# Probabilities times values in two halves around the state and output updates of the middle stage

## The chip, the cores and the metric

The kernel runs on one core of one Trainium2 chip. Its time is the device time of one execution in microseconds (us). The profile names five engines: PE (TensorE, with PEld for its weight loads), DVE (VectorE), ACT (ScalarE), POOL (GpSimd) and SP (SyncE, which only issues transfers here).

## What is computed

One layer of a streaming encoder: a layer norm, an input projection, two groups of heads side by side, an output projection with a layer norm, and an MLP with another. The change touches the place where the two groups of heads share TensorE. Cut to that:

```python
# (a) gated delta rule, per head: state S, blocks of tokens
u = U_c - jnp.einsum('bhck,bhkv->bhcv', W_c, S)
o = jnp.einsum('bhck,bhkv->bhcv', qd_c, S) + jnp.einsum('bhij,bhjv->bhiv', qk_c, u)
S = gt_c[..., None, None] * S + jnp.einsum('bhck,bhcv->bhkv', kd_c, u)
# (b) attention over a sliding window, with a sink per head
s = jnp.einsum('bnqhgd,bnshd->bnhgqs', q, k).astype(jnp.float32) * SWA_HD ** -0.5 + bias
p = jax.nn.softmax(jnp.concatenate([s, sink], axis=-1), axis=-1)[..., :-1]
return jnp.einsum('bnhgqs,bnshd->bnqhgd', p.astype(v.dtype), v)
# then o is normalised per head and gated; both groups are concatenated
h = layer_norm(DEEP_ALPHA * h + mix @ w_o, ln1_g, ln1_b)
```

Sizes: 2048 prompt tokens, 16 meta tokens and 32 sample tokens, 8 heads of width 64 in each group, model width 1024, everything float32.

## The kernel before

Three stages follow each other: the projection (`project_stage`, to about 690 us), the middle stage (`mix_stage`, to about 1420 us) and the MLP (`mlp_stage`, the rest). The middle stage walks over 18 tiles of 128 tokens. Each engine has a function `step(t)`, which lists its work for tile t in a fixed order, and `over_tiles` runs it: four tiles written out, then a hardware loop of two tiles a turn, then four more. Tile 17 holds the sample tokens. An engine does its list strictly in this order. Between engines stand semaphores: `pe.wait_ge(s["u_done"], ...)` holds TensorE until VectorE has written `u`.

The tiles are skewed. While tile t goes through the delta rule, the next tile n = t + 1 is prepared (gates, decays, scores) and the tile before, p = t - 1, gets its output product and layer norm. So one `step(t)` of TensorE runs: the gates and transposes of n; `turn_o(p)` (the transposes of the normalised `o` of tile p, which wait for `on_done`); `turn_queries(n)`; half of the output product of p; `from_state(t)`; and so on down to the part that matters here:

- `scores(n)` (L1109): scores of the next tile, into the banks `fr` and `inv`.
- `solve_rest(t)` (L1181): the last step of the triangular solve, into `one1`.
- `attend(t)` (L1232): probabilities times values of the 8 heads, two matmuls a head, into the bank `pair`.
- `state_update(t)` (L1188), which waits for `u_done`, and `output_update(t)` (L1194), which has the same input `u`, into `one1` and `one2`.
- `turn_attention(t)` (L1239): 4 transposes of the scaled attention, which wait for `attn_scaled`.
- `turn_values(n)` (L1118): 2 transposes of the next tile's values into `one2`, which wait for `o_done`, since `one2` must have been read.
- then the next step begins with `turn_gates` (L1032).

VectorE at the same place: `biased(n)` (L1458, 8 heads, waits for the scores), `update(t)` (L1519 writes `u`, then L1520), `maxima(n)`, `norm_stats(p)`, `new_state(t)` (L1530), `scale_attention(t)` (L1565, waits for `pv_full`, which `attend` gives), `norm_shift(p)` (L1589), `new_output(t)` (L1525, waits for `oin_full`, which `output_update` gives, and gives `o_done`). Its next step begins with `copy_gates`, `copy_sums` (L1386 to L1394) and `sum_squares` (L1535).

ScalarE: `norm_rstd(p)`, `normalise(p)` (L1797, waits for `norm_shift`), `square_o(t)` (L1765, waits for `o_done`), `mix_attention(t)` (L1777, waits for `turn_attention`), `split_attention(t)` (L1783), `copy_values(n)` (L1749).

In the steps of tiles 0 and 16 `maxima(n)` also hides keys (`hide`, L1465 and L1473), which takes VectorE some 5 us more.

Of the kernel before, what the change touches and what calls it, by code (L numbers as in the profile page):

```python
# [35 lines left out]
HEADS, HD = 8, 64  # L36
# [677 lines left out]
def by(t, per, k=None):  # L714

    return t.n * per + (per if k is None else k)
# [12 lines left out]
def mix_stage(nc, ctx, io, project):  # L729
# [69 lines left out]
    def heads4(ps, n=P):  # L799
        return ps[:, :].rearrange("p (h c) -> p h c", c=n)  # L800
# [22 lines left out]
    s = {n: m.sem(n) for n in names}  # L823
# [16 lines left out]
    def following(t):  # L840

        return None if t.last() else t.plus(1)
# [179 lines left out]
    def _(pe):  # L1022
# [30 lines left out]
        def turn_queries(t):  # L1053
            if t.reaches(2):
                pe.wait_ge(s["attn_mixed"], by(t.plus(-2), 1))
            pass_waits(pe, s["passed"])
            turn_rows(t, pair, 0, s["q_turned"])
# [54 lines left out]
        def turn_values(t):  # L1112
            if t.reaches(1):
                pe.wait_ge(s["o_done"], by(t.plus(-1), 1))
            else:
                pe.wait_ge(*project.evacuated)
            for j in range(2):
                last = pe.transpose(one2[:, j * P:j * P + P], values[:, j * P:j * P + P], ident)  # L1118
            last.then_inc(s["vwin_turned"], 1)
# [97 lines left out]
                last = pe.transpose(out, probs[:, h, j * P:j * P + P], ident)  # L1217
            last.then_inc(s["pt_full"], 1)

        def attend(t):  # L1220
            pe.wait_ge(s["vwin_copied"], by(t, 1))
            pe.wait_ge(s["pt_copied"], by(t, 2))
            if t.reaches(2):
                pe.wait_ge(s["h1t_copied"], by(t.plus(-2), 2))
            elif t.reaches(1):
                pe.wait_ge(s["attn_mixed"], by(t.plus(-1), 1))
            if not t.last():
                pe.wait_ge(s["squared"], by(t.plus(1), 2))
            for h in range(HEADS):
                kv = h // 4  # L1230
                for j in range(2):
                    last = pe.matmul(pair[:, h * HD:h * HD + HD], probs_t[:, j, h, :], v_rows[:, j, kv * HD:kv * HD + HD],  # L1232
                                     start=j == 0, stop=j == 1)
            last.then_inc(s["pv_full"], 1)

        def turn_attention(t):
            pe.wait_ge(s["attn_scaled"], by(t, 1))
            for j in range(4):
                last = pe.transpose(pair[:, j * P:j * P + P], attn[:, 2 * j:2 * j + 2, :].rearrange("p a b -> p (a b)"), ident)  # L1239
            last.then_inc(s["ost_full"], 1)  # L1240
# [35 lines left out]
        def step(t):  # L1276
            n, p, pp = following(t), t.plus(-1), t.plus(-2)
            chain, norm = t.reaches(1), t.reaches(2)
            if n:
                turn_gates(n)  # L1280
                turn_rows(n, inv[1], 4, s["k_turned"])
                turn_rows(n, inv[0], 8, s["v_turned"])
                sum_gates(n)
                mask_future(n)
                spread_gates(n)
            if chain:
                turn_o(p)
            if n:
                turn_queries(n)
            if chain:  # L1290
                output_product(p, 0, ATTENTION, n)
            if n:
                key_products(n)
            from_state(t)
            if chain:
                output_product(p, 0, DELTA)
            if n:
                query_products(n)
            if chain:
                output_product(p, 1, ATTENTION)  # L1300
            if norm:
                turn_h1(pp, 0, n)
            turn_probs(t, 0)
            pair_rows(t)
            turn_probs(t, 1)
            pair_update(t)
            if norm:
                turn_h1(pp, 1)
            if chain:
                output_product(p, 1, range(0, 2))  # L1310
            solve_head(t)
            if chain:
                output_product(p, 1, range(2, 4))
            carry_over(t)
            if n:
                scores(n)
            solve_rest(t)
            attend(t)
            state_update(t)
            output_update(t)  # L1320
            turn_attention(t)
            if n:
                turn_values(n)

        def first_turns():
            relative_bias()
# [36 lines left out]
    def _(dve):  # L1363
# [158 lines left out]
        def new_output(t):  # L1522
            dve.wait_ge(s["oin_full"], by(t, 1))
            dve.wait_ge(s["qs_scaled"], by(t, 2))
            dve.tensor_tensor(o[:, :, :], o[:, :, :], heads4(one2, HD), ALU.add).then_inc(s["o_done"], 1)  # L1525
# [36 lines left out]
        def scale_attention(t):  # L1562
            dve.wait_ge(s["pv_full"], by(t, 1))
            dve.wait_ge(s["soft_end"], by(t, 2))
            dve.tensor_tensor(attn[:, :, :], heads4(pair, HD), across(soft[:, 5, :], HD), ALU.mult).then_inc(s["attn_scaled"], 1)  # L1565
# [39 lines left out]
        def step(t):  # L1605
            n, p = following(t), t.plus(-1)
            chain = t.reaches(1)
            if n:
                copy_gates(n)
                copy_sums(n)  # L1610
            if chain:
                sum_squares(p)
                low(p, ATTENTION, 1)
                normalise_o(p)
            if n:
                sum_keys(n)
            if chain:
                gate_o(p)
            if t.reaches(2):
                norm_gain(t.plus(-2))  # L1620
            if n:
                strengths(n)
                scale_values(n)
            if chain:
                low(p, DELTA, 2)
            if n:
                decayed_keys(n)
            residue(t)
            if chain:
                residual(p, 0)  # L1630
            if n:
                left_keys(n)
                decayed_queries(n)
                sum_queries(n)
            turn_even(t)
            copy_pair_rows(t)
            place_pair(t)
            if chain:
                residual(p, 1)
            take_over(t)  # L1640
            softmax_sums(t)
            if n:
                biased(n)
            update(t)
            if n:
                maxima(n)
            if chain:
                norm_stats(p)
            new_state(t)
            scale_attention(t)  # L1650
            if chain:
                norm_shift(p)
            new_output(t)
            if not chain:
                for k in DELTA:
                    split_wo(k)
# [32 lines left out]
    def _(act):  # L1689
# [57 lines left out]
        def copy_values(t):  # L1747
            act.wait_ge(s["vwin_turned"], by(t, 1))
            act.activation(v_rows[:, :, :], one2[:, 0:SPAN].rearrange("p (a c) -> p a c", c=P), ACT.Copy).then_inc(s["vwin_copied"], 1)  # L1749
# [13 lines left out]
        def square_o(t):  # L1763
            act.wait_ge(s["o_done"], by(t, 1))
            act.activation(o_sq[:, :, :], o[:, :, :], ACT.Square).then_inc(s["o_squared"], 1)  # L1765
# [7 lines left out]
        def mix_attention(t):  # L1773
            act.wait_ge(s["ost_full"], by(t, 1))
            if t.reaches(1):
                act.wait_ge(s["mix_lo_done"], by(t.plus(-1), 2, 1))
            act.activation(mixed[:, 4:8, :], heads4(pair), ACT.Copy).then_inc(s["attn_mixed"], 1)  # L1777
# [26 lines left out]
        def step(t):  # L1804
            n, p, pp = following(t), t.plus(-1), t.plus(-2)
            chain, norm = t.reaches(1), t.reaches(2)
            if n:
                square_keys(n)
            if chain:
                rstd_o(p)  # L1810
            if n:
                decays(n)
                key_norms(n)
            if chain:
                split_delta(p)
            if n:
                square_queries(n)
            probabilities(t, range(0, 3))
            if n:
                to_lanes(n)  # L1820
            probabilities(t, range(3, HEADS))
            if n:
                query_norms(n)
            if norm:
                copy_h1(pp, 0)
            copy_probs(t, 0)
            copy_probs(t, 1)
            if norm:
                copy_h1(pp, 1)
            copy_head(t)  # L1830
            if chain:
                norm_rstd(p)
                normalise(p)
            square_o(t)
            mix_attention(t)
            split_attention(t)
            if n:
                copy_values(n)
            if not chain:
                for k in DELTA:  # L1840
                    split_wo(k)
# [531 lines left out]
```

## Time and profile before

| | |
|---|---|
| median of 3 runs | 2953.55 us (2951.76 to 2960.93) |
| the profiled execution, its own time | 2953.84 us |
| its span | 2952.0 us |
| PE busy | 2743.6 us, 93% |
| DVE, ACT, POOL busy | 44%, 31%, 45% |
| mean granted clock of TensorE | 0.964 |

The page shows one execution. Busy shares are means over stages, so the stretch of the middle stage is read by itself: the waits of one engine, and the instructions of each engine in order of time. In a row of the timeline the first number is the start, the second the time to the end of the last instruction of the group, and the brackets hold the idle time ahead of it and what ended it. A group of matmuls ends a little after the next one starts, because matmuls overlap. Every product of two float32 operands here has two records, so 16 records are 8 products.

### The profile page before, as it was taken

The page shows a single profiled execution, that of the slowest core. Times are in us where ns is not written, and L with a number is a line of the kernel's source. Part 1 is how long each engine was busy: PE and PEld are TensorE (multiplying, and loading weights), DVE is VectorE, ACT ScalarE, POOL GpSimd, SP SyncE. Part 2 cuts the span into 40 slices and gives each one's busy share as a digit, 9 for nine tenths or more (in the row PEclk, how much of TensorE's full clock was granted, in tenths as well). Part 3 has the DMA queues.
Part 4 walks back from the last instruction along what each step waited for, and adds up shares of the span by engine and source line. Part 5 has one row for each costly group of instructions (what it writes and reads, how often), then busy time and mean ns, then how long its engine had stood idle before and what let it go on. Part 6 is the DMA issues. An engine that isn't in the chain of part 4 may idle for free.

```text
span 2952.0 us, 50987 instructions
## 1 busy us (share of the span) xinstructions
PE 2743.6 (93%) x17652; PEld 2600.4 (88%) x17652; DVE 1287.8 (44%) x2442; ACT 922.6 (31%) x1966; POOL 1333.6 (45%) x1840
## 2 busy tenths in 40 slices
PE   5899988977999999998599999999999999999996
PEld 5799988966888877887499999999999999999996
DVE  7634420016766667765344126413641364136402
ACT  4322241113444444443122222222222222222222
POOL 4200003002555544553255555555555555555553
PEclk9899999986999999998799999999999999999998
DMA  5322243232343333332334434443443344434433
GB/s 195 122 93 70 70 91 88 69 134 76 96 111 106 106 105 96 96 105 73 112 118 139 125 111 136 152 125 112 135 151 125 114 135 150 126 115 136 140 116 86
DMA packets 225941, 336.70 MB, mean 114 GB/s; under 512 B 78426, under 2 KB 161562, under 8 KB 223018
## 3 DMA queue, kind: packets, MB, share of 16 engines
q1 hardware_dynamic: 205210, 331.44, 36.5%
q10 hardware_dynamic: 20640, 4.07, 0.7%
q8 instruction: 54, 0.88, 0.1%
q14 instruction: 37, 0.30, 0.0%
HBM read 265.67 MB, written 69.78 MB: 114 GB/s over the span
## 4 chain that ended last, share of the span: by engine, by line
PE 50%; DVE 1%; DMA 0%; issue 0%; ACTq 0%; DVEq 0%
PE c_bank L128 16%; PE c_bank L130 16%; PE c_bank L129 16%; PE c_turned L2088 1%; DMA c_out<-scratch_h_cols 0%; DVE c_stats L2212 0%; DVE c_raw L2209 0%; DVE c_h_lo L2254 0%; DVE c_out L2248 0%; DVE c_raw L2261 0%; DVE c_h_hi L2252 0%; DVE c_raw L2264 0%; DVE c_mean_var L2215 0%; ACTq L2133 0%; DVEq L2248 0%
## 5 line engine op out<-in xcount | busy, mean ns | idle before, releaser
L2123 POOL TENSOR_TENSOR c_w_lo<-c_raw,c_w_hi 128x512 fp32r<-128x512 f32 x640 | 852.8, 1333 | 641.7 <-ACT c_w_hi L2143 641.7
L2143 ACT ACTIVATE c_w_hi<-c_raw 128x512 fp32r<-128x512 f32 x640 | 404.4, 632 | 1056.9 <-PE c_bank L130 1025.1
L128 PE MATMUL c_bank<-c_h_hi,c_w_hi 128*128 128x416 f32 x1280 | 453.6, 354 | 24.8 <-POOL c_w_lo L2123 23.0
L130 PE MATMUL c_bank<-c_h_hi,c_w_lo 128*128 128x416 f32 x1280 | 452.2, 353 | 0.0
L130 PE MATMUL c_bank<-c_mid_hi,c_w_lo 128*128 128x416 f32 x1280 | 450.8, 352 | 0.0
L128 PE MATMUL c_bank<-c_mid_hi,c_w_hi 128*128 128x416 f32 x1280 | 450.2, 352 | 0.0
L129 PE MATMUL c_bank<-c_h_lo,c_w_hi 128*128 128x416 f32 x1280 | 448.6, 350 | 0.0
L129 PE MATMUL c_bank<-c_mid_lo,c_w_hi 128*128 128x416 f32 x1280 | 447.0, 349 | 0.0
L2248 DVE COPY c_out<-c_bank 128x416 f32 x40 | 23.7, 591 | 627.3 <-PE c_bank L130 627.3
L1895 POOL TENSOR_TENSOR b_lane_t<-b_lane_a,b_lane_n 128x60 f32<-128x60 f32 (+24 forms) x558 | 160.2, 287 | 297.3 <-DMA b_lane_a<-scratch_at_lanes 255.0
L128 PEld LDWEIGHTS c_bank<-c_h_hi,c_w_hi 128*128 128x128 f32 x1280 | 241.4, 189 | 27.1 <-POOL c_w_lo L2123 24.6
L130 PEld LDWEIGHTS c_bank<-c_h_hi,c_w_lo 128*128 128x128 f32 x1280 | 241.3, 189 | 3.3
L129 PEld LDWEIGHTS c_bank<-c_h_lo,c_w_hi 128*128 128x128 f32 x1280 | 241.1, 188 | 2.8
L130 PEld LDWEIGHTS c_bank<-c_mid_hi,c_w_lo 128*128 128x128 f32 x1280 | 240.2, 188 | 3.2
L129 PEld LDWEIGHTS c_bank<-c_mid_lo,c_w_hi 128*128 128x128 f32 x1280 | 240.0, 188 | 2.8
L128 PEld LDWEIGHTS c_bank<-c_mid_hi,c_w_hi 128*128 128x128 f32 x1280 | 240.4, 188 | 0.1
L567 POOL TENSOR_TENSOR a_w_lo<-a_raw,a_w_hi 128x1024 fp32r<-128x1024 f32 x20 | 48.2, 2412 | 393.2 <-ACT a_w_hi L586 393.2
L2195 DVE TENSOR_SCALAR c_positive<-c_bank 128x416 f32<-128x416 f32 x160 | 94.4, 590 | 242.9 <-PE c_bank L130 242.9
L128 PE MATMUL a_one<-a_h_hi,a_w_hi 128*128 128x420 f32 (+1 forms) x480 | 171.1, 356 | 15.3 <-ACT a_row L613 15.3
L1898 POOL TENSOR_TENSOR b_lane_n<-b_lane_n,b_lane_t 128x60 f32<-128x60 f32 (+24 forms) x558 | 159.2, 285 | 43.7
L129 PE MATMUL a_one<-a_h_lo,a_w_hi 128*128 128x420 f32 (+1 forms) x480 | 170.3, 355 | 0.0
L130 PE MATMUL a_one<-a_h_hi,a_w_lo 128*128 128x420 f32 (+1 forms) x480 | 170.3, 355 | 0.0
(277 smaller groups left out, 4654.2 us busy)
## 6 DMA issues: line engine op xcount, KB each, us to landing
c_raw<-in_w_ff SPq DMA_DIRECT2D x320, 512.0 KB, 3.7
scratch_proj<-a_row SPq DMA_DIRECT2D x22, 1152.0 KB, 5.1
b_qkv<-scratch_proj SPq DMA_DIRECT2D x18, 768.0 KB, 6.5
a_raw<-in_w_in SPq DMA_DIRECT2D x23, 512.0 KB, 5.9
a_x<-in_x SPq DMA_DIRECT2D x18, 512.0 KB, 3.6
scratch_h_rows<-a_h SPq DMA_DIRECT2D x18, 512.0 KB, 2.7
b_lane_a<-scratch_at_lanes SPq DMA_DIRECT2D x72, 128.0 KB, 2.7
b_res<-scratch_h_rows SPq DMA_DIRECT2D x18, 512.0 KB, 3.3
```

Of the source, the lines that this page charges most:

```text
L128: pe.matmul(out, w_hi, x_hi, start=first, stop=False)
L129: pe.matmul(out, w_hi, x_lo, start=False, stop=False)
L130: return pe.matmul(out, w_lo, x_hi, start=False, stop=last)
L567: pool.tensor_tensor(w_lo[:, p, :, :], raw[:, p, :, :], w_hi[:, p, :, :].bitcast(F32), ALU.subtract).then_inc(w_lo_done, 1)
L1895: pool.tensor_tensor(term, lane_a[:, j, j + 1:SMALL].unsqueeze(1).to_broadcast(shape), lane_n[:, 0:n, j].unsqueeze(2).to_broadcast(shape), ...
L1898: last = pool.tensor_tensor(here, here, term, ALU.add)
L2088: last = pe.transpose(turned[p][0:TOK, c * P:c * P + P], out[:, c, i * TOK:i * TOK + TOK], ident[:, :])
L2123: pool.tensor_tensor(w_lo[:, p % 2, ks, :], raw[:, p, ks, :], w_hi[:, p % 2, ks, :].bitcast(F32), ALU.subtract).then_inc(w_lo_done, 1)
L2143: act.activation(w_hi[:, p % 2, ks, :], raw[:, p, ks, :], ACT.Copy).then_inc(w_hi_done, 1)
L2195: dve.tensor_scalar(positive[:, :], src, 0.0, None, ALU.max).then_inc(positive_done, 1)
L2248: dve.tensor_copy(out[:, one(c2 * 2 + c), :], bank2[c][:, 0:BLOCK].unsqueeze(1)).then_inc(out_done, 1)
```

## The change

TensorE does heads 0 to 3 of `attend` ahead of `state_update`, and heads 4 to 7 behind `output_update`. All waits of `attend` stand ahead of the first half; `pv_full` is given by the second. `turn_values` moves ahead of `turn_attention`. VectorE does `new_output` right behind `new_state`, and `scale_attention` last in the step. ScalarE does `copy_values` ahead of `mix_attention`.

```diff
-        def attend(t):
-            pe.wait_ge(s["vwin_copied"], by(t, 1))
-            pe.wait_ge(s["pt_copied"], by(t, 2))
-            if t.reaches(2):
-                pe.wait_ge(s["h1t_copied"], by(t.plus(-2), 2))
-            elif t.reaches(1):
-                pe.wait_ge(s["attn_mixed"], by(t.plus(-1), 1))
-            if not t.last():
-                pe.wait_ge(s["squared"], by(t.plus(1), 2))
-            for h in range(HEADS):
+        def attend(t, heads):
+            if heads[0] == 0:
+                pe.wait_ge(s["vwin_copied"], by(t, 1))
+                pe.wait_ge(s["pt_copied"], by(t, 2))
...
+            for h in heads:
...
-            last.then_inc(s["pv_full"], 1)
+            if heads[-1] == HEADS - 1:
+                last.then_inc(s["pv_full"], 1)
...
-            attend(t)
+            attend(t, range(0, 4))
             state_update(t)
             output_update(t)
-            turn_attention(t)
+            attend(t, range(4, HEADS))
             if n:
                 turn_values(n)
+            turn_attention(t)
...
             new_state(t)
-            scale_attention(t)
+            new_output(t)
             if chain:
                 norm_shift(p)
-            new_output(t)
+            scale_attention(t)
...
             square_o(t)
+            if n:
+                copy_values(n)
             mix_attention(t)
             split_attention(t)
-            if n:
-                copy_values(n)
```

On TensorE, at the end of a step inside the loop, from the last score to the first transposes of the next step (the line numbers shift by one or two in the changed kernel):

```order
 L1109 MATMUL a_inv<-b_keys,b_sq 128x256
 L1181 MATMUL a_one<-b_rn,b_nn_1005 64x64 x8
-L1232 MATMUL a_pair<-b_v_rows,b_probs_t 128x64 x16
+L1233 MATMUL a_pair<-b_v_rows,b_probs_t 128x64 x8
 L1188 MATMUL a_one<-b_u,b_kd_1010 64x64 x8
 L1194 MATMUL a_one<-b_u,b_qk_1008 128x64 x8
-L1239 MATMUL a_pair<-b_masks,b_turned_rows 128x128 x4
+L1233 MATMUL a_pair<-b_v_rows,b_probs_t 128x64 x8
 L1118 MATMUL a_one<-b_masks,b_values 128x128 x2
+L1241 MATMUL a_pair<-b_masks,b_turned_rows 128x128 x4
 L1032 MATMUL a_prod<-b_masks,b_gate_rows 128x16
```

Half of the attention's matmuls now stand between the output update and the value transposes, and the attention transposes (L1239, now L1241) come last.

VectorE at the end of the same step, before:

```order
311 L1519 TENSOR_TENSOR b_u<-a_one,b_neg_beta 128x512
312 L1520 TENSOR_TENSOR b_state<-b_state,b_e_end 128x256
...
316 L1585 BN_AGGR b_mean_var<-b_stats 128x2
317 L1530 TENSOR_TENSOR b_state<-b_state,a_one 128x256
318 L1565 TENSOR_TENSOR b_turned_rows<-a_pair,b_soft 128x512
319 L1589 SCALAR_TENSOR_TENSOR b_small<-b_mean_var,b_small 128x1
320 L1525 TENSOR_TENSOR b_o<-b_o,a_one 128x512
321 L1386 COPY b_gate<-a_prod 128x2x8
```

and in the changed kernel, where every line number of VectorE is three higher:

```order
311 L1522 TENSOR_TENSOR b_u<-a_one,b_neg_beta 128x512
312 L1523 TENSOR_TENSOR b_state<-b_state,b_e_end 128x256
...
316 L1588 BN_AGGR b_mean_var<-b_stats 128x2
317 L1533 TENSOR_TENSOR b_state<-b_state,a_one 128x256
318 L1528 TENSOR_TENSOR b_o<-b_o,a_one 128x512
319 L1592 SCALAR_TENSOR_TENSOR b_small<-b_mean_var,b_small 128x1
320 L1568 TENSOR_TENSOR b_turned_rows<-a_pair,b_soft 128x512
321 L1389 COPY b_gate<-a_prod 128x2x8
```

The new output (L1525, now L1528) and the scaled attention (L1565, now L1568) have changed places; what writes `u` has the 8 instructions of `biased(n)` ahead of it in both.

## Rows read from the trace of the kernel before

**Rows 1.** The page: PE's busy time, its share of the span, instructions.

```profile
PE 2743.6 (93%) x17652; PEld 2600.4 (88%) x17652; DVE 1287.8 (44%) x2442; ACT 922.6 (31%) x1966; POOL 1333.6 (45%) x1840
```

**Rows 2.** Waits of PE, 780 to 1300 us: total, times, longest.

```profile
PE a_one L1201 <- DVE b_turned_rows L1546: 15.0, 13, 1.2
PE a_one L1118 <- DVE b_o L1525: 4.4, 13, 0.3
PE a_fr L1071 <- DVE b_cum L1394: 3.8, 13, 0.3
```

**Rows 3.** Timeline of PE, end of one step: start, length, line [idle before].

```profile
1028.49 1.14 PE L1181 MATMUL a_one<-b_rn,b_nn 64*64 64x64 f32 x16
1029.56 3.79 PE L1232 MATMUL a_pair<-b_v_rows,b_probs_t 128*128 128x64 f32 x32
1033.27 0.97 PE L1188 MATMUL a_one<-b_u,b_kd 128*64 128x64 f32 x16
1034.17 2.00 PE L1194 MATMUL a_one<-b_u,b_qk 128*128 128x64 f32 x16
1036.00 0.61 PE L1239 MATMUL a_pair<-b_masks,b_turned_rows 128*128 128x128 f32 x4
1036.95 0.44 PE L1118 MATMUL a_one<-b_masks,b_values 128*128 128x128 f32 x2 [0.34 <-DVE b_o L1525]
1037.32 0.23 PE L1032 MATMUL a_prod<-b_masks,b_gate_rows 16*128 16x16 f32 x1
...
1041.98 0.66 PE L1201 MATMUL a_one<-b_masks,b_turned_rows 128*128 128x128 f32 x4 [1.11 <-DVE b_turned_rows L1546]
```

**Rows 4.** Timeline of DVE, the same step.

```profile
1028.77 0.48 DVE L1458 CUSTOM_DVE_ANT_0 b_probs<-a_fr,b_bias,b_sinks 128x256 f32<-128x256 f32 x1 [0.98 <-PE a_inv L1109]
...
1032.02 0.69 DVE L1519 TENSOR_TENSOR b_u<-a_one,b_neg_beta 128x512 f32<-128x512 f32 x1
...
1034.89 0.40 DVE L1530 TENSOR_TENSOR b_state<-b_state,a_one 128x256 f32<-128x256 f32 x1
1035.21 0.68 DVE L1565 TENSOR_TENSOR b_turned_rows<-a_pair,b_soft 128x512 f32<-128x512 f32 x1
1035.81 0.15 DVE L1589 SCALAR_TENSOR_TENSOR b_small<-b_mean_var,b_small 128x1 f32<-128x1 f32 x1
1036.20 0.69 DVE L1525 TENSOR_TENSOR b_o<-b_o,a_one 128x512 f32<-128x512 f32 x1 [0.25 <-PE a_one L1194]
...
1039.48 0.68 DVE L1535 TENSOR_REDUCE b_o_sum<-b_turned_rows 128x8 f32<-128x512 f32 x1
```

**Rows 5.** Timeline of ACT, the same step.

```profile
1035.99 1.24 ACT L1797 ACTIVATE b_x<-b_x,b_small 128x1024 f32<-128x1024 f32 x1 [0.45 <-DVE b_small L1589]
1037.14 0.61 ACT L1765 ACTIVATE b_turned_rows<-b_o 128x512 f32<-128x512 f32 x1
...
1038.34 0.63 ACT L1783 ACTIVATE b_mix_hi<-b_mixed 128x512 fp32r<-128x512 f32 x1
```

**Rows 6.** Timeline of PE, the attention transposes in tiles 0 and 16.

```profile
712.63 1.08 PE L1239 MATMUL a_pair<-b_masks,b_turned_rows 128*128 128x128 f32 x4 [2.80 <-DVE b_turned_rows L1565]
...
1356.00 1.12 PE L1239 MATMUL a_pair<-b_masks,b_turned_rows 128*128 128x128 f32 x4 [4.55 <-DVE b_turned_rows L1565]
```

**Rows 7.** Windows of PE: stretch, us, busy (instructions), granted clock, DMA share, GB/s.

```profile
840.00:850.00 10.00, 8.78 (x80) 0.83 0.25 48
...
1280.00:1290.00 10.00, 10.00 (x76) 0.86 0.21 31
```

**Rows 8.** Timeline of PE, first output product of two tiles and what follows.

```profile
1002.80 0.75 PE L128 MATMUL a_prod<-b_wo_hi,b_mix_hi 128*128 128x512 f32 x1
...
1007.32 1.16 PE L1081 MATMUL a_fr<-b_qkv 64*128 64x128 f32 x16
...
1042.83 0.48 PE L128 MATMUL a_prod<-b_wo_hi,b_mix_hi 128*128 128x512 f32 x1
...
1045.77 1.16 PE L1081 MATMUL a_fr<-b_qkv 64*128 64x128 f32 x16
```

More of the change, by code:

```diff
@@ L1218, in turn_probs @@
             last.then_inc(s["pt_full"], 1)
-        def attend(t):
-            pe.wait_ge(s["vwin_copied"], by(t, 1))
-            pe.wait_ge(s["pt_copied"], by(t, 2))
-            if t.reaches(2):
-                pe.wait_ge(s["h1t_copied"], by(t.plus(-2), 2))
-            elif t.reaches(1):
-                pe.wait_ge(s["attn_mixed"], by(t.plus(-1), 1))
-            if not t.last():
-                pe.wait_ge(s["squared"], by(t.plus(1), 2))
-            for h in range(HEADS):
+        def attend(t, heads):
+            if heads[0] == 0:
+                pe.wait_ge(s["vwin_copied"], by(t, 1))
+                pe.wait_ge(s["pt_copied"], by(t, 2))
+                if t.reaches(2):
+                    pe.wait_ge(s["h1t_copied"], by(t.plus(-2), 2))
+                elif t.reaches(1):
+                    pe.wait_ge(s["attn_mixed"], by(t.plus(-1), 1))
+                if not t.last():
+                    pe.wait_ge(s["squared"], by(t.plus(1), 2))
+            for h in heads:
                 kv = h // 4
```

## The prediction

> **What bounds the kernel now.** The page comes first: TensorE is busy for 93% of the span, every other engine for less than half [rows 1]. So time comes only out of TensorE's gaps, and is lost wherever it gets a new one. The waits of TensorE in 13 middle tiles come second [rows 2]: `turn_o` waits 15.0 us in all (1.15 us a tile) for the normalised `o`; `turn_values` 4.4 us (0.34) for `o_done`; `spread_gates` 3.8 us (0.29). There is nothing else. In particular there is no wait for `u_done` and none for `attn_scaled`. The timeline tells why [rows 3, 4]. The last score is followed by VectorE's `biased`, from 1028.77 to 1032.02, and `u` is written from 1032.02 to 1032.71. TensorE is meanwhile in `attend`, from 1029.56 to 1033.27, 3.71 us long. `u` is there 0.56 us before TensorE asks for it: `attend` is the cover for `biased` and `u`, and nearly all of it is needed.
>
> **The change part by part**, for one tile in the middle (tiles 1 to 15 run alike), on the clock times of [rows 3, 4]. The matmuls are the same, so only waits are to be found.
>
> First half of `attend`: half of 3.71 is 1.85 us, so it ends at 1031.41. `u` is ready at 1032.71, and from the end of `new_output` at 1036.89 to the start of L1118 at 1036.95 a release takes 0.06, so `state_update` starts at 1032.77. That is a new wait of 1.36 us, which the 0.56 us of slack don't cover. Everything behind it in TensorE's queue stands still.
>
> State update 0.90 us (1033.27 to 1034.17) and output update 1.83 us (1034.17 to 1036.00), so they end at 1035.50, 0.50 us sooner than before. Second half of `attend`: 1.85 us, to 1037.35. `new_output` needs the output update's last result (2.00 us after its start, 1035.67) and VectorE, which is free at 1035.3 behind `new_state` (its input comes at about 1033.7, and L1530 is held till 1034.89 by the statistics, as before). So it runs from 1035.70 to 1036.39, and `turn_values` no longer waits: the 0.34 us are gone. It takes 0.37 us (1036.95 to 1037.32), to 1037.72.
>
> `turn_attention` now waits for `scale_attention`, which waits for the second half. Its last result comes some 0.16 us after TensorE could go on (2.00 against 1.83), at 1037.51; VectorE starts 0.03 later, takes 0.68 us [rows 4] and is seen 0.06 later: 1038.28. TensorE has been idle since 1037.72, a second new wait of 0.56 us. Before, the scaling was over at 1035.89, when TensorE was still in the output update. The transposes take about 0.44 us, so the next step's `turn_gates` starts at 1038.72 instead of 1037.32: **1.40 us later**. As a sum of gaps: 1.36 + 0.56 - 0.34 = 1.58, of which the earlier 0.34 is measured from the end of a group and not from where the next could start (0.5 us from there: 1036.95 less 1036.44); start to start it is 1.40, which I keep.
>
> Does the rest of the step give it back? The one large wait is `turn_o`'s. It waits for a chain that begins at VectorE's L1535. That instruction starts at 1039.48, right behind `copy_sums`, although its input, the squares, was ready at 1037.75 [rows 5]. So the chain hangs on the gates of the next tile, which TensorE itself starts, and moves with them by 1.40 us. That `o` is ready sooner brings nothing. ScalarE's part gets later and stays covered: `norm_shift` now stands behind `new_output`, so `normalise` starts at about 1036.5 instead of 1035.99, the squares are ready at 1038.25 instead of 1037.75, and L1535 would now start at 1040.9. `copy_values` (0.3 us) ahead of `mix_attention` fills a time in which that one waits anyway: it can start only at 1038.9, `split_attention` ends at about 1040.1, and VectorE takes the low part only behind L1535, so after 1041.6. The next `copy_gates` finds VectorE free since 1038.22. No transfer is moved; no queue of SP or POOL is passed.
>
> The other tiles. In steps 0 and 16 VectorE is 5 us late by `hide`, and TensorE waits for it at the attention's transposes [rows 6]. The halves move inside these 2.80 and 4.55 us. The new order adds the 0.6 us of L1525 ahead of the scaling, but `turn_values` goes in ahead of it and covers that: 0 for tile 0, 0.3 us for tile 16. Tile 17 has no `biased`, so `u` comes in time; its attention ends 0.1 us later. Sum: 15 x 1.40 + 0.4 = **21.4 us**.
>
> **The clock** is the open term. The granted clock falls to its lower level (1.2 instead of 2.4 GHz) for a short stretch after `turn_o`'s wait in 8 of the 15 tiles: 8 stretches between 740 and 1340 us, of which the windows of the first and the last stand in [rows 7]. Its price: from the first output matmul to `key_products` one such tile takes 4.52 us, one at full clock 2.94 [rows 8], so 1.58 us. The old waits stay as they are and come 1.4 us later, so the 8 can become anything from 0 to 15: -12.6 to +11.1 us. The new wait of 1.36 us is about as long as `turn_o`'s (1.1 to 1.2), after which the clock does fall in half the cases. But `turn_o`'s has a second wait (L1071) shortly ahead of it [rows 2], and the new one stands between dense matmuls. It can cost a second stretch in 0 to 15 tiles, 0 to 23.7 us. Of all this I take three stretches more, 4.7 us, near the lower end, because the nearest rows with a single gap don't show it.
>
> Total: 2953.84 + 21.4 + 4.7 = 2980 us. The profiled execution is 0.3 us from the median of the runs, so no correction.
>
> One rule from outside speaks on the price of a wait. The trace shows at L1118 that the transposes' first weights were loaded when the wait ended, not during it: both start at 1036.95, as they must if the wait stands ahead of both. The Trainium skill, page "TensorE: Matmul & The Clock Gate", section "Step-by-step: what each phase is for", says that TensorE pulls weight loads ahead of matmuls still in flight. If that also passed a semaphore wait, each of the two new waits would be cheaper by one load, at the page's P / 1.2 some 0.1 us (an estimate), and the sum smaller by 3 us. By this trace it doesn't.
>
> **The rivals.**
> *The clock falls in nearly every tile behind the new wait.* For: its length. Against: the dense work on both sides. With 12 to 15 more stretches instead of 3 the sum is 21.4 + 19 to 24: 2994 to 2999 us. Chance 0.18.
> *`u` comes sooner than by the row.* Its place is `biased`: if its eight instructions ran faster while TensorE did less beside them, and `u` were there by 1031.41 (1.30 us sooner, which is the point from which this decides), the step would be 0.90 + 1.83 + 1.85 + 0.16 + 0.03 + 0.68 + 0.06 + 0.44 from there: 1037.36, +0.04 us a tile, 2955 us. Half of it gives 2965. Against: the eight take 0.41 us each from 1028.77 to 1032.02, and no row shows that TensorE slows them. Chance 0.07.
> *`turn_o` follows the output update instead of the gates.* Then the earlier `o` counts, the wait of 1.11 us a tile goes, and with it the fall of the clock behind it: 21.4 - 16.6 - 12.6 = -7.8, 2946 us. It decides if L1535 is held by the squares. The rows show it held by the queue. Chance 0.03.
> *The half behind the output update doesn't land where it should*, since its results and the scaling lie in one bank and ScalarE gets late by more than I count: another 0.5 us a tile, 2987 us. Chance 0.07.
>
> **How the numbers follow.** The forecast has a chance of 0.65, with its own range of 2968 to 2990 (21.4 with 5 fewer up to 9 more stretches). To hold the time 8 times in 10, the range takes in most of the clock rival: 2966 to 2996. A measurement here can tell about 0.3% (9 us) from no change, so "slower" begins at 2962.4: forecast, clock rival, late half, and half of the second rival, 0.91. Within 0.3%: 0.07. Faster: 0.02.
>
> **What the new profile would show.** A wait of TensorE at the state update for `u` of 1.2 to 1.4 us in 15 tiles; one at the attention's transposes for the scaling of 0.4 to 0.6 us; none at `turn_values`; `turn_o` unchanged at 1.1 to 1.2. No wait for `u` would make the first step wrong; a shorter `turn_o` wait the claim on the chain. The count of stretches at half clock decides the last term.

## The result and the profile after

The changed kernel takes 3060.34 us (median of 4 runs, 3048.28 to 3070.0) against 2957.24 (2951.76 to 2966.41): a ratio of **1.0343, interval 1.0296 to 1.0391**. Slower, as forecast, but by 103 us where 26 were forecast, and outside the range. The profiled execution is the slowest of the four, 3070.0 us.

The waits of TensorE in the whole middle stage (where, waited for whom, total, times, longest):

```profile
PE a_one L1188 <- DVE b_u L1522: 19.9, 17, 1.2
PE a_one L1201 <- DVE b_turned_rows L1549: 16.1, 17, 3.1
...
PE a_pair L1241 <- DVE b_turned_rows L1568: 6.7, 17, 0.8
...
PE a_one L1118 <- DVE b_o L1528: 0.3, 1, 0.3
```

Two waits are new and one is gone, as the step by step working said: for `u` (L1188), for the scaled attention (L1241), and no longer for `o_done` at L1118 [rows 2]. `turn_o` (L1201) waits 1.0 to 1.2 us in 10 of the tiles 1 to 15, as before, and less in the others. The two new ones are 27 us, so waits are not where 103 us went. The timeline of TensorE over the end of one step, to be read beside [rows 3]:

```profile
1033.98 2.00 PE L1233 MATMUL a_pair<-b_v_rows,b_probs_t 128*128 128x64 f32 x16
1037.17 1.60 PE L1188 MATMUL a_one<-b_u,b_kd 128*64 128x64 f32 x16 [1.19 <-DVE b_u L1522]
1038.70 3.68 PE L1194 MATMUL a_one<-b_u,b_qk 128*128 128x64 f32 x16
1042.17 3.62 PE L1233 MATMUL a_pair<-b_v_rows,b_probs_t 128*128 128x64 f32 x16
1045.59 0.63 PE L1118 MATMUL a_one<-b_masks,b_values 128*128 128x128 f32 x2
1046.58 1.12 PE L1241 MATMUL a_pair<-b_masks,b_turned_rows 128*128 128x128 f32 x4 [0.36 <-DVE b_turned_rows L1568]
1047.62 0.28 PE L1032 MATMUL a_prod<-b_masks,b_gate_rows 16*128 16x16 f32 x1
...
1053.64 1.07 PE L1201 MATMUL a_one<-b_masks,b_turned_rows 128*128 128x128 f32 x4 [1.22 <-DVE b_turned_rows L1549]
```

From start to start, the state update takes 1.53 us (0.90 before), the output update 3.47 (1.83), the second half of the attention 3.42 (1.85 by half of before). From the state update to `turn_gates` it is 10.45 us; the forecast had 5.95. Windows of the same stretch (us, busy and instructions of PE, granted clock, DMA share, GB/s) show the reason:

```profile
1033.00:1036.00 3.00, 2.98 (x32) 1.00 0.21 86
1036.00:1039.00 3.00, 1.83 (x18) 0.61 0.00 0
1039.00:1042.00 3.00, 3.00 (x16) 0.50 0.00 0
1042.00:1045.00 3.00, 3.00 (x16) 0.50 0.00 0
1045.00:1048.00 3.00, 2.64 (x12) 0.50 0.09 25
1048.00:1051.00 3.00, 2.97 (x14) 0.61 0.65 171
1051.00:1054.00 3.00, 1.52 (x18) 0.95 0.22 33
1054.00:1057.00 3.00, 3.00 (x12) 0.50 0.22 33
1057.00:1060.00 3.00, 3.00 (x25) 0.98 0.00 0
```

The clock falls to half in the wait for `u` and stays there over all that follows, 13.7 us, into the gates of the next tile. It falls once more behind `turn_o`'s wait. A long stretch comes in 14 of the tiles 1 to 15 (not in tile 3). It begins between 0.5 us before and 2.0 us after the start of the state update and lasts 10.2 to 20.5 us; in 8 of the 14 tiles a second, short one of 3.4 us follows. A tile takes 46.5 us on average instead of 39.5. Counts and lengths of stretches, here and below, are read from the granted clock over tiles 1 to 15 of the one profiled execution of each kernel; the windows shown are examples. Over the same 600 us the mean granted clock is 0.83 against 0.98 in the kernel before:

```profile
740.00:1340.00 600.00, 566.26 (x4819) 0.83 0.32 87
```

Where the time of such a tile goes, start to start, in us:

| part of the tile | before | after | forecast |
|---|---|---|---|
| start of the attention to start of the state update | 3.71 | 3.19 | 3.21 |
| state update to `turn_gates` | 4.05 | 10.45 | 5.95 |
| `turn_gates` to `turn_o` | 4.66 | 6.02 | 4.66 |

### The profile page after: what moved, and what is told of

Same layout as the page of the kernel before. It is cut to its first block and busy times, and to the rows that moved or that the text cites. A ratio compares the mean times of both kernels' runs of the same rounds, so it can differ in the third digit from the quotient of the medians.

```text
span 3068.2 us, 50987 instructions
## 1 busy us (share of the span) xinstructions
PE 2853.2 (93%) x17652; PEld 2698.7 (88%) x17652; DVE 1289.9 (42%) x2442; ACT 927.5 (30%) x1966; POOL 1331.8 (43%) x1840
```

## The experiments

Theory A: TensorE's idleness in the wait for `u` makes the clock fall, and the light work behind it (matmuls of 64 columns, each behind its own weight load, and transposes) keeps it low. Theory B: the light work, now in one piece, makes it fall however long the wait is. Theory C: the wait at the attention's transposes does it. All ratios are to the kernel before on the same chip, which took 2953 to 2961 us; so kernels of different groups are compared by their ratios.

**Six heads ahead, two behind.**

```diff
-            attend(t, range(0, 4))
+            attend(t, range(0, 6))
...
-            attend(t, range(4, HEADS))
+            attend(t, range(6, HEADS))
```

> The changed kernel with 6 heads ahead of the state update and 2 behind the output update. The same matmuls and the same order otherwise; only the wait for u gets shorter, from 1.2 us (shown) to about 0.3, since 2.78 us of attention cover it instead of 1.85. Theory A (the wait for u makes the clock fall, and the light work behind it keeps it low): no fall at the state update, some 7 us over the kernel before by the waits alone, 2961 to 2966 us, ratio to before about 1.002 to 1.004. Theory B (the clock falls because the light matmuls now lie in one piece with the transposes, however long the wait is): still 3040 to 3060 us. Theory C (it is the wait at the attention's transposes, which stays at 0.4 to 0.6 us here): also above 3030 us.

Measured: 2974.35 us, ratio 1.0073 (1.0056 to 1.009). Waits of TensorE, 780 to 1300 us (where, for whom, total, times, longest):

```profile
PE a_one L1201 <- DVE b_turned_rows L1549: 15.0, 13, 1.2
PE a_pair L1241 <- DVE b_turned_rows L1568: 6.0, 13, 0.5
PE a_one L1188 <- DVE b_u L1522: 3.9, 13, 0.3
```

The wait for the scaling is still there, 0.5 us a tile, the wait for `u` is 0.3, and the clock falls at the state update in none of the 15 tiles. That is against C and B. The time is 8 us above the range expected, 2961 to 2966, and the ratio above its 1.004: the short stretches behind `turn_o` rose from 8 to 12 tiles, which the expectation had left out.

**The new order without the split.**

```diff
-            attend(t, range(0, 4))
+            attend(t, range(0, HEADS))
             state_update(t)
             output_update(t)
-            attend(t, range(4, HEADS))
```

> All 8 heads ahead of the state update as before, but the rest of the change kept: new output ahead of the scaled attention, value transposes ahead of the attention's, the value copy first on ScalarE. It shows what the new order costs without the split. Wait for u: none. The attention's transposes wait for the scaling, which now comes 0.7 us later: +0.7 us a tile, 10 us, 2964 to 2968 us. Theory A: no long stretch at half clock, ratio about 1.003 to 1.005. Theory B and C: long stretches here too, since the light work and the wait at the transposes are both there, above 3030 us.

Measured: 2982.14 us, ratio 1.0092 (1.0075 to 1.0109), above my 2964 to 2968. The waits are 0.8 us a tile at the value transposes and 0.2 at the attention's. The expectation had only 0.7 at the attention's; it did not say that the value transposes, now ahead, wait for `o_done`. And the short stretch behind `turn_o` comes in all 15 tiles, with one more in tile 1. There is no long stretch: against B, and less strongly against C, whose wait is only 0.2 us here. So even the order by itself is a loss.

**`u` ahead of the biased scores.** The layer norm's statistics go ahead with it.

```diff
-            if n:
-                biased(n)
-            update(t)
-            if n:
-                maxima(n)
             if chain:
                 norm_stats(p)
+            update(t)
+            if n:
+                biased(n)
+                maxima(n)
```

> The changed kernel with 4 and 4 heads, but VectorE does the layer norm's statistics and the update (which writes u) ahead of the biased scores. u is then there 0.7 us after the solve, at about a third of the first half of the attention, so the wait for u is gone; the biased scores end 0.7 to 0.9 us later, ahead of where they are needed. Theory A: no fall at the state update; the step is as long as before to 0.1 us, 2955 to 2965 us, ratio 1.000 to 1.003. Theory B or C: 3030 us and more.

Measured: 2968.0 us, ratio 1.0049 (1.0033 to 1.0066), 3 us above the range expected. Waits of TensorE, 780 to 1300 us:

```profile
PE a_one L1201 <- DVE b_turned_rows L1549: 15.0, 13, 1.2
PE a_pair L1241 <- DVE b_turned_rows L1568: 7.3, 13, 0.6
PE a_fr L1071 <- DVE b_cum L1397: 3.7, 13, 0.3
```

The split is as in the changed kernel, the wait for `u` is gone, and with it the long stretches: none in 15 tiles. What is left is the wait at the attention's transposes (0.6 us, now the only new wait) and short stretches in 10 tiles instead of 8.

**Work in place of the wait.**

```diff
+        def fill(p):
+            pe.wait_ge(s["resid_done"], by(p, 2))
+            for k in range(5):
+                pe.matmul(prod[:, :], mix_hi[:, 0, :], wo_hi[:, 0, 0:512], start=True, stop=True)
...
             attend(t, range(0, 4))
+            if chain:
+                fill(p)
             state_update(t)
```

> The changed kernel with 5 matmuls of 512 columns put between the first half of the attention and the state update, about 1.15 us of work whose result is never read, in tiles 1 to 17. The wait for u turns into work of the same length, and nothing else moves. Theory A (it is TensorE's idleness there): the clock keeps up at the state update and what is left is the pure delay that was forecast, 21 us: 2972 to 2980 us, ratio 1.006 to 1.009. Theory B (the light work behind it is enough): 3045 to 3065 us, as without the filling.

Measured: 2982.57 us, ratio 1.0099 (1.0083 to 1.0116). That is 3 us above the range expected, and by the ratios some 72 us less than the changed kernel, with more work in it. TensorE's timeline in one tile:

```profile
1046.69 2.00 PE L1233 MATMUL a_pair<-b_v_rows,b_probs_t 128*128 128x64 f32 x16
1048.50 1.40 PE L1241 MATMUL a_prod<-b_wo_hi,b_mix_hi 128*128 128x512 f32 x5
1049.89 0.97 PE L1188 MATMUL a_one<-b_u,b_kd 128*64 128x64 f32 x16
1050.79 2.00 PE L1194 MATMUL a_one<-b_u,b_qk 128*128 128x64 f32 x16
1052.62 1.95 PE L1233 MATMUL a_pair<-b_v_rows,b_probs_t 128*128 128x64 f32 x16
1054.41 0.39 PE L1118 MATMUL a_one<-b_masks,b_values 128*128 128x128 f32 x2
1055.36 0.66 PE L1246 MATMUL a_pair<-b_masks,b_turned_rows 128*128 128x128 f32 x4 [0.56 <-DVE b_turned_rows L1575]
1055.94 0.23 PE L1032 MATMUL a_prod<-b_masks,b_gate_rows 16*128 16x16 f32 x1
```

The state update starts 3.20 us after the attention, as in the changed kernel (3.19), so the data moves as there. But the clock is at full height through the updates, and they take 0.90 and 1.83 us. No tile of the 15 has a long stretch; 10 have the short one behind `turn_o`. From the attention to the gates it is 9.25 us; the prediction had 9.16. Its windows (columns as above):

```profile
1048.00:1052.00 4.00, 4.00 (x39) 1.00 0.00 0
1052.00:1056.00 4.00, 3.44 (x31) 1.00 0.00 0
1056.00:1060.00 4.00, 3.23 (x32) 1.00 0.57 148
1060.00:1064.00 4.00, 3.39 (x12) 0.57 0.30 46
```

Here dense work stands in the place of the idleness; with six heads ahead, and with `u` first, the idleness is gone and nothing dense was put in. The clock holds in all three. Together they settle that it is idleness, and not the order, that makes the clock fall at the state update.

**The wait without the split.** On the kernel before:

```diff
             if n:
                 biased(n)
-            update(t)
-            if n:
                 maxima(n)
             if chain:
                 norm_stats(p)
+            update(t)
```

> The kernel before, undivided attention and its own order, with one edit: VectorE writes u behind the maxima and the layer norm's statistics instead of ahead of them, 1.8 us later. TensorE then waits about 1.3 us for u (a gap of 1.1 to 1.2 us as the profile counts it), with no split. Theory A (the wait makes the clock fall, the light work behind it keeps it low up to the next output product): half clock from the state update on in most of the tiles, 10 to 14 us long, 3020 to 3050 us, ratio 1.023 to 1.033. Rival (only together with the split, with its second half of the attention behind, does the clock stay low): a fall of 3.4 us at most, 20 us of waits and 24 of clock, below 3000 us.

Measured: 3015.66 us, ratio 1.0195 (1.0177 to 1.0214), below the 3020 to 3050 of theory A and above the rival's 3000. The clock falls at the state update in 12 of 15 tiles, so a wait of about 1.3 us (1.2 to 1.4 in these 12 but for one of 1.6) is enough, split or not. Windows of one tile, whose state update starts at 1061.4:

```profile
1060.00:1063.00 3.00, 1.74 (x25) 1.00 0.00 0
1063.00:1066.00 3.00, 3.00 (x16) 0.50 0.00 0
1066.00:1069.00 3.00, 3.00 (x15) 0.50 0.21 62
1069.00:1072.00 3.00, 2.42 (x21) 0.86 0.63 149
```

But the stretch is 6.8 us in 10 of these tiles and 13.7 in 2. The expectation of 10 to 14 us was wrong, and so was its rival of 3.4. In the ten tiles the clock comes back 1.6 to 4.2 us after `turn_gates` starts; in the changed kernel, where the stretch is 10.2 or 13.7 us, 2.7 to 4.3 us after it. So it comes back at about the same place of the program, but without the second half of the attention that place comes sooner, and the fall itself comes 0.8 to 2.2 us after the update's start. By this reading, which no run tests alone, the split costs twice: it opens the wait, and it puts more light work behind it.

**Five heads ahead, three behind.** As the first diff, with 5 for 6.

> The changed kernel with 5 heads ahead and 3 behind: a wait for u of about 0.9 us (shown as 0.7), between that of 6 heads (shown 0.3, no fall) and that of 4 (shown 1.2, a fall in nearly every tile). If the fall comes with the length of the wait, gradually: falls at the state update in some tiles and 2985 to 3030 us. If it needs a wait near 1.2 us: none, and 14 us of delay plus what the stretches behind the normalised o cost with 6 heads: 2975 to 2985 us.

Measured: 2994.55 us, ratio 1.0107 (1.0085 to 1.0129), as expected for a fall that comes by degrees. A wait for `u` of 0.7 to 0.8 us made the clock fall at the state update in 3 of 15 tiles, and then for 13.7, 20.5 and 20.5 us; such a tile takes 45 to 47 us, one of the others 39.5 to 42.7. So the fall comes with the wait's length by degrees: 0 of 15 tiles at 0.3 us, 3 at 0.7, 14 at 1.2. The 3 were counted in the slowest of four executions; the others took 2984 to 2995 us, and no trace shows their falls.

**Dense work behind the state update.** The changed kernel with `fill` of 8 matmuls between the two updates; the wait for `u` is left.

```diff
             state_update(t)
+            if chain:
+                fill(p)
             output_update(t)
```

> The changed kernel, 4 and 4 heads, the wait for u left as it is, with 8 matmuls of 512 columns (never read) between the state update and the output update. They cost 1.8 us at full clock and 3.4 at half. Theory A (the clock falls by the wait, and stays low because what follows is light): it still falls in nearly every tile, but the stretch is 3.4 to 6.8 us instead of 13.7, and in spite of the added work the time is 3000 to 3035 us, below the changed kernel. Rival (the stretch has a length of its own, whatever work follows): 13.7 us as before, and 3080 us or more.

Measured: 3033.11 us, ratio 1.0248 (1.0231 to 1.0265), as expected by theory A, and by the ratios some 28 us less than the changed kernel although it does more. The clock still falls at the state update, in 14 of 15 tiles, but for 3.4 us in 12 of them and 6.8 in 2. One of the 12:

```profile
1026.00:1029.00 3.00, 2.16 (x18) 0.65 0.00 0
1029.00:1032.00 3.00, 3.00 (x16) 0.78 0.00 0
1032.00:1036.00 4.00, 3.44 (x31) 1.00 0.00 0
```

So the length of the stretch is no fixed price. It is set by what TensorE does at the low clock: 3.4 us with eight matmuls of 512 columns in it, 13.7 with light ones. And the light work behind the filling ran at full clock (last window), so light work alone does not bring the clock down.

**Only one of the two large waits.** The changed kernel, with the squares of `o` summed earlier:

```diff
             if n:
                 copy_gates(n)
-                copy_sums(n)
             if chain:
                 sum_squares(p)
+            if n:
+                copy_sums(n)
+            if chain:
                 low(p, ATTENTION, 1)
```

> The changed kernel with the squares of o summed early (between the gate copies), so that the wait for the normalised o falls from 1.2 to about 0.3 us, and the wait for u stays at 1.2. If the wait for u alone starts the stretch at half clock and light work carries it: it still falls in nearly every tile, 10 to 14 us long, and the time is the changed kernel's less 13 us or a little more: 3035 to 3050 us, ratio 1.025 to 1.03. If the two waits together made it (the clock kept down by the second): stretches of 6.8 us or less and 3000 us or below.

Measured: 3021.38 us, ratio 1.0222 (1.02 to 1.0243). By the ratios that is some 36 us less than the changed kernel, where 13 or a little more were expected. `turn_o` waits 0.3 us or less instead of 1.2, and the stretch at the state update is still there in 12 of 15 tiles, 10.2 us in 4 and 13.7 in 8. So it needs the wait for `u` alone. What is gone are the second, short stretches, which 8 tiles of the changed kernel had behind a long one, and the long ones of 17 and 20 us, which 4 had: these came with the other wait.

**The same edit on the kernel before, and on the split without its wait.**

> The kernel before with one edit: VectorE sums the squares of o between its copies of the gates and of their sums, in a gap of 1.2 us in which it waits, instead of behind them. The chain to the normalised o gets about 0.85 us shorter, so the one large wait of TensorE falls from 1.1 to 0.3 us a tile: 13 us. If the falls of the clock behind that wait (8 of 15 tiles, 1.6 us each) are due to it, they go too: 2928 to 2935 us, ratio 0.992 to 0.994. If they stay: 2940 us. If ScalarE's logarithm and exponential for o come no sooner, since it transposes squares first: 2950 us.

Measured: 2938.45 us, ratio **0.9923 (0.9903 to 0.9942)**: faster than both kernels, and the ratio is in the range expected (the time is 3 us above it, since the kernel before took 2961 us in this group). In the kernel before VectorE sat idle for 1.2 us between the two groups of copies:

```profile
1039.00 0.29 DVE L1391 COPY b_cum_row<-a_prod 72x128 f32<-72x128 f32 x1 [1.17 <-PE a_prod L1063]
```

Now it does the sum (L1535) there, right behind the gate copies:

```profile
1030.65 0.18 DVE L1386 COPY b_gate<-a_prod 128x16 f32<-128x16 f32 x1 [0.69 <-PE a_prod L1032]
1030.74 0.16 DVE L1387 COPY b_beta<-a_prod 128x8 f32<-128x8 f32 x1
1030.81 0.68 DVE L1535 TENSOR_REDUCE b_o_sum<-b_turned_rows 128x8 f32<-128x512 f32 x1
1031.52 0.18 DVE L1538 TENSOR_TENSOR b_o_sum<-b_o_sum,b_q_scale 128x8 f32<-128x8 f32 x1
1032.07 0.29 DVE L1391 COPY b_cum_row<-a_prod 72x128 f32<-72x128 f32 x1 [0.36 <-PE a_prod L1063]
```

TensorE then waits 0.27 us at `turn_o`, and the clock holds between 780 and 1300 us:

```profile
1034.21 0.66 PE L1201 MATMUL a_one<-b_masks,b_turned_rows 128*128 128x128 f32 x4 [0.27 <-DVE b_turned_rows L1546]
```

```profile
780.00:1300.00 520.00, 502.99 (x5124) 1.00 0.40 110
```

The eight short stretches of the kernel before [rows 7] are gone with the wait of [rows 2]. A tile takes 38.0 us instead of 39.5. Summed up, 15 x 1.48 is 22 us, and 22 show.

The second kernel has the edits of `u` ahead of the biased scores and of the early sum together:

> The split of 4 and 4 heads with neither of the large waits: u written ahead of the biased scores, and the squares of o summed early. It tells whether the split is worth anything once its wait is gone. By the waits it is as long as the undivided kernel with the early sums plus the 0.5 us a tile at the attention's transposes less the 0.3 at the value transposes: 2938 to 2945 us, ratio 0.992 to 0.995, no better than the undivided one. If the split itself helps: below 2935 us.

Measured: 2943.31 us, ratio 0.9946 (0.9925 to 0.9967), as expected. With both large waits gone the split costs nothing that can be told from the undivided kernel's 0.9923 (the intervals overlap, and the two were not run beside each other), and brings nothing: a tile takes 38.3 us instead of 38.0.

## Why the prediction was wrong

- *The wait for `u`*: right. 1.36 us forecast from start to start; the state update starts 3.19 us after the attention, 3.21 forecast. In the trace it is 1.2 us in tiles 1 to 16. Tile 0 waits too, 0.8 us; its time at half clock becomes one stretch of 27.3 us instead of 13.7 in two, and it takes 3.4 us more, where the forecast had 0.
- *The wait at the attention's transposes* (0.56) and the end of that at `turn_values`: right. At full clock, in the kernel with filling, it is 0.56, as forecast. In the changed kernel it is mostly shorter, since TensorE is slower ahead of it.
- *`turn_o` gains nothing by the earlier `o`*: right. With filling it waits 1.1 to 1.2 us in each tile, as before; in the changed kernel it waits 1.0 to 1.2 us in 10 of 15 tiles and less in the others, where TensorE itself comes late to it at half clock. That its chain hangs on the queue and not on the squares was then confirmed by moving the sum.
- *The delay of 1.40 us a tile, 21.4 us*: right as a term. With filling a tile without any low stretch takes 39.9 us, 1.45 more than the 38.46 before. Where such a tile ends a turn of the hardware loop it takes 40.35 us, 1.25 more than the 39.1 before.
- *The clock, 4.7 us*: this step failed, by both its factors. The **count**: I took three more stretches, because the new wait "stands between dense matmuls". It does not: attention and updates are matmuls of 64 columns, and the clock fell to half in 14 of 15 tiles. The **price**: I took 1.58 us from [rows 8], where the clock is low over matmuls of 512 columns and comes back after 3.4 us. Behind the state update it stays low for 13.7 us in most tiles. In the tile shown the updates, the half attention and the transposes behind it cost 4.5 us more than forecast, the gates 1.4, and the output product behind `turn_o` up to 1.6 again. A tile with a fall takes 45.2 to 47.7 us, one with filling and no stretch 39.9 to 40.4: 5 to 8 us a fall instead of 1.58. The term is 103 less 21.4, some 80 us, instead of 4.7. My clock rival had the mechanism and a chance of 0.18, but the same price, so its 2999 was 61 us short as well. The direction was no luck: it follows from the wait for `u`, which came as forecast.
- *The chances*: those that I added up to "slower" come to 0.93, not to 0.91. That changes nothing in the forecast.
- *The rule on weight loads* was read rightly here: the first load of the state update starts at 1037.17 with its matmul, when the wait ends (columns as in the timeline, weight loads of the changed kernel, in the row below). The Trainium skill ("TensorE: Matmul & The Clock Gate", "Step-by-step: what each phase is for") speaks of loads pulled ahead of matmuls in flight; here the load doesn't pass the semaphore wait, as the prediction read it at L1118.

```profile
1037.17 1.41 PEld L1188 LDWEIGHTS a_one<-b_u,b_kd 128*64 128x64 f32 x16 [1.33 <-DVE b_u L1522]
```

What stays open: why 1.2 us of waiting makes the clock fall in 14 tiles at the state update and in 8 to 15 behind `turn_o`, depending on the variant. The same wait for `u` of 1.2 us, with the short wait at `turn_o`, gave 12 tiles. No run here separates the length of the wait from its place and the work right ahead of it.

## What to carry to other kernels

Before work is taken off the front of a queue, ask what it covers: here the attention covered VectorE's 4 us between the scores and `u` with 0.56 us to spare, and half of it was not enough. A wait of TensorE of 1.2 us cost 5 to 8 us a tile here with light work behind it, so a forecast has to price the clock with the work that will run in the low stretch, not with a stretch measured elsewhere. And read the large waits of the kernel at hand first: one reordered sum on VectorE, in a gap where it idled, gave 0.8%.

## What was not expected of the hardware

- A wait of 1.2 us brings the granted clock from 2.4 to 1.2 GHz in 14 of 15 tiles (12 when the wait at `turn_o` is short), one of 0.7 in 3, one of 0.3 in none.
- The low stretch was the longer, the more light work stood in it: mostly 13.7 us with matmuls of 64 columns and transposes, mostly 6.8 with less of them, mostly 3.4 with eight matmuls of 512 columns behind the first update.
- Five matmuls whose results nobody reads, put into each wait, saved some 72 us of the changed kernel's time.
